# Two chunks of the up projection multiplied before the layer norm ahead of them, and corrected afterwards

## What is computed

```
x = layer_norm(x, ln_in_g, ln_in_b)
for l in range(2):
    ...                                           # four mixers side by side give ym
    x = layer_norm(ALPHA * x + (1 + g1) * (ym @ w_out[l]), ln1_g[l], ln1_b[l])
    h = x * (1 + sc2) + sh2
    a = depthwise_conv3(h @ w_up[l], conv_w[l]) + conv_b[l]     # w_up: 1024 x 5632
    val, gate = split(a)
    x = layer_norm(ALPHA * x + (1 + g2) * ((val * silu(gate)) @ w_down[l]), ln2_g[l], ln2_b[l])
```

## Time and profile before

| | |
|---|---|
| median of three runs | 1433.19 us |
| profiled execution | 1431.97 us |
| its span, first to last instruction | 1429.9 us |
| TensorE busy | 1358.1 us, 95% |
| VectorE, ScalarE, GpSimd busy | 772.3, 505.8, 537.4 us |
| mean granted TensorE clock | 0.965 |

### The profile page before, as it was taken

One profiled execution on the slowest core, in us unless ns is written; L12 is line 12 of the kernel. 1 busy time (PEld: TensorE's weight loads), 2 busy tenths in 40 slices (PEclk: granted clock), 3 DMA queues, 4 the chain that ended last, 5 costly groups with the idle time before them and its releaser, 6 DMA issues.

```text
span 1429.9 us, 17219 instructions
## 1 busy us (share of the span) xinstructions
PE 1358.1 (95%) x6876; PEld 1013.5 (71%) x6876; DVE 772.3 (54%) x1366; ACT 505.8 (35%) x762; POOL 537.4 (38%) x325
## 2 busy tenths in 40 slices
PE   6999999999999999899899999999999999989987
PEld 3445676787888888688665577677788888868865
DVE  5985778646676676432468655664533333321135
ACT  2523225335333333332242422343543333333222
POOL 0630100575444444344346110056544444434431
PEclk9998999999999999999999999999999999999998
DMA  9356732032565555454224441102133333222311
GB/s 382 148 118 163 174 124 90 16 103 90 181 200 190 186 184 179 160 182 156 106 64 118 85 81 30 45 16 88 59 89 103 89 92 100 89 73 90 102 59 59
DMA packets 64799, 166.78 MB, mean 117 GB/s; under 512 B 14288, under 2 KB 26960, under 8 KB 64208
## 3 DMA queue, kind: packets, MB, share of 16 engines
q1 hardware_dynamic: 64720, 165.68, 38.1%
HBM read 160.04 MB, written 5.62 MB: 116 GB/s over the span
## 4 chain that ended last, share of the span: by engine, by line
PE 79%; DVE 14%; issue 3%; DMA 2%; POOL 1%; ACT 1%; SPq 1%; ACTq 0%; POOLq 0%
PE bank L449 19%; PE bank L451 19%; PE bank L450 19%; PE bank L530 6%; PE bank L524 3%; PE bank L555 2%; PE bank L464 2%; PE bank L469 1%; DVE scr L1237 1%; DVE xa L1044 1%; PE bank L683 1%; DVE xa L1038 1%; DMA s_w<-scr 1%; PE bank L458 1%; PE bank L692 1%
## 5 line engine op out<-in xcount | busy, mean ns | idle before, releaser
L2083 POOL TENSOR_TENSOR ring_r<-ring,scr_r 128x1024 fp32r<-128x1024 f32 x148 | 360.2, 2435 | 442.0 <-ACT scr_r L1950 272.8
L449 PE MATMUL bank<-ym_r,scr_r 128*128 128x512 f32 x704 | 280.2, 398 | 5.1 <-DVE hm_r L1600 4.1
L451 PE MATMUL bank<-hm_r,scr_r 128*128 128x512 f32 x704 | 279.4, 397 | 0.0
L450 PE MATMUL bank<-ym_r,ring_r 128*128 128x512 f32 x704 | 276.7, 393 | 0.0
L449 PE MATMUL bank<-scr_r 128*128 128x512 f32 x480 | 197.2, 411 | 28.7 <-issue 14.2
L450 PE MATMUL bank<-scr_r,ring_r 128*128 128x512 f32 x480 | 191.3, 399 | 0.0
L1616 DVE SCALAR_TENSOR_TENSOR scr<-bank,pb,scr 128x511 f32<-128x511 f32 x88 | 66.0, 750 | 211.9 <-ACT scr L1943 211.8
L530 PE MATMUL bank<-hm,ring 128*128 128x512 f32 x352 | 171.7, 630 | 0.0
L1099 DVE SCALAR_TENSOR_TENSOR ada<-ada,silu_c 128x1024 f32<-128x1024 f32 x80 | 134.2, 1680 | 50.5 <-DMA ada<-in_w_ada 50.5
L449 PEld LDWEIGHTS bank<-ym_r,scr_r 128*128 128x128 f32 x704 | 132.3, 188 | 38.7 <-issue 5.7
L451 PEld LDWEIGHTS bank<-hm_r,scr_r 128*128 128x128 f32 x704 | 132.3, 188 | 33.0
(11 more groups left out here) (332 smaller groups left out, 1791.2 us busy)
## 6 DMA issues: line engine op xcount, KB each, us to landing
ring<-in_w_up SPq DMA_DIRECT2D x88, 512.0 KB, 3.7
ada<-in_w_ada SPq DMA_DIRECT2D x80, 512.0 KB, 3.7
ring<-in_w_down SPq DMA_DIRECT2D x44, 512.0 KB, 3.6
ring<-in_w_in SPq DMA_DIRECT2D x34, 512.0 KB, 4.5
scr<-in_w_ada SPq DMA_DIRECT2D x16, 512.0 KB, 14.5
ring<-in_w_out SPq DMA_DIRECT2D x16, 512.0 KB, 4.2
pa<-in_par_a SPq DMA_DIRECT2D x2, 2144.5 KB, 12.9
xa<-in_x SPq DMA_DIRECT2D x1, 2048.0 KB, 8.3
```

Source lines behind the costliest of these rows:

```text
L449: first = mm(dst, w_hi, x_hi, start=start, stop=False)
L450: mm(dst, w_lo, x_hi, start=False, stop=False)
L451: return first, mm(dst, w_hi, x_lo, start=False, stop=stop)
L2083: G.tensor_tensor(ring_r[:, at, :], ring[:, at, :], high[:, at, :].bitcast(F32), ALU.subtract)\
```

## The change

The product with w_up is linear in h, and h = (xa * rstd - mean * rstd) * g + b for each frame. So a chunk of it can be made from the stream as it is ahead of the norm, times g, and corrected later: multiplied by the spread row rstd, less the spread row mean * rstd times the column sums of g * w, plus the column sums of b * w.

- `zh` (ScalarE) and `z_low` (VectorE) split xa * g into its two halves, a slice at a time, right behind `residual`. The square of each slice comes behind `zh`, and `z_low` waits for that square.
- `weigh` (VectorE) multiplies up chunks 0 and 1 by g and by b, after slice 5; `collect` adds the eight slices of each: chunk 0 after slice 6, ahead of residual 7; chunk 1 ahead of `norm_apply`. GpSimd makes the low part of these two chunks, in place, only after `weigh` has read them.
- TensorE runs `norm_stats`, raw slices 0 and 1 of the pair, the spreads, raw slices 2 to 6, four one-column matmuls for the sums, raw slice 7. All `keep_awake` of this norm are gone. Then chunks 2 and 3 form the pair that goes slice by slice as h comes.
- ScalarE makes the high part of up chunk 3 ahead of the norm's square root, copies the raw results out of banks 2 and 3 between h's slices 2, 3 and 4, and makes those of chunks 4 and 5 among and behind h's slices.
- VectorE makes the low part of chunk 4 and the corrections behind `norm_apply`; ScalarE adds one bias instruction ahead of the first tap of each raw chunk.

```diff
+                def raw_slice(k):
+                    pe.wait_ge(S["raw_step"], l * NRAW + RAW[f"z{k}"])
+                    for r, (w_hi, w_lo) in enumerate(raw_pair):
+                        first, last = thrice(banks[2 + r][:, :], w_hi[:, k, :], w_lo[:, k, :], zh[:, k, :],
+                                             z_low_tile(k), k == 0, k == KD - 1)
+                        if k == 0 and r == 0:
+                            first.then_inc(S["chunk_used"], 1)
...
+                for k in range(KD):
+                    pe.wait_ge(S["h_lo_odd" if k % 2 else "h_lo"], l * (KD // 2) + k // 2 + 1)
+                    for r, (w_hi, w_lo) in enumerate(pair):
+                        first, last = thrice(banks[4 + r][:, :], w_hi[:, k, :], w_lo[:, k, :], ym_r[:, k, :],
+                                             hm_r[:, k, :], k == 0, k == KD - 1)
+                        if k == 0 and r == 0:
+                            first.then_inc(S["chunk_used"], 2)
...
+                def z_low(k):
+                    v.wait_ge(S["ln_sq"], (2 * l + 1) * KD + k + 1)
+                    V.scalar_tensor_tensor(z_low_tile(k), xa[:, k, :], gh[:, 1, 0, k:k + 1], zh[:, k, :].bitcast(F32),
+                                           ALU.mult, ALU.subtract).then_inc(S["raw_step"], 1)
+                def weigh(r):
...
+                    for x in range(2):
+                        ins = V.tensor_tensor(weighed[r][:, x, :, :], ring[:, slot(l, n), :].rearrange("p (k m) -> p k m", m=P),
+                                              gh[:, 1, x, :].rearrange("p (k o) -> p k o", o=1).to_broadcast([P, KD, P]), ALU.mult)
+                    ins.then_inc(S["raw_step"], 1)
+                def collect(r):
+                    a = weighed[r]
+                    ch.link(V.tensor_tensor(a[:, :, 0:4, :], a[:, :, 0:4, :], a[:, :, 4:8, :], ALU.add))
+                    ch.link(V.tensor_tensor(a[:, :, 0:2, :], a[:, :, 0:2, :], a[:, :, 2:4, :], ALU.add))
+                    V.tensor_tensor(columns[:, r, :, :], a[:, :, 0, :], a[:, :, 1, :], ALU.add).then_inc(S["raw_step"], 1)
...
                     norm_square((2 * l) * KD, m, m)
+                weights_high(l, KD + 3)
                 norm(2 * l + 2)
...
+                    if k in (2, 3):
+                        a.wait_ge(S["up_mm"], l * (2 * KF) + 2)
+                        A(up_raw[:, k - 2, :], banks[k][:, :], ACT.Identity)
+                    if k == 5:
+                        weights_high(l, KD + 4)
+                weights_high(l, KD + 5)
...
+                    if q in (KD, KD + 1):
+                        g.wait_ge(S["raw_step"], l * NRAW + RAW[f"weighed{q - KD}"])
```

More of the change, by code:

```diff
@@ L109 @@
 TAIL = 4
+RAW = {name: i + 1 for i, name in enumerate(
+    [f"z{k}" for k in range(6)] + ["weighed0", "weighed1", "z6", "sum0", "z7", "sum1", "low", "up0", "up1"])}
+NRAW = len(RAW)
 PA = [("gm_g", GW), ("gm_b", GW), ("gm_ws", HEADS * P), ("gm_bs", CT * P),
@@ L495, in norm_stats, with norm_pause @@
                     last.then_inc(S["ln_bcast"], 1)
+            def norm_pause(n, late=None):
+                norm_stats(n, late)
+                keep_awake(1)
+                norm_spread(n)
                 keep_awake(2)
@@ L508, in _ @@
             last.then_inc(S["ln_accq"], 1)
-            norm_stats(1)
+            norm_pause(1)
             for l in range(L):
@@ L959, in _ @@
                 pe.wait_ge(S["up_conv"], l * (2 * KF) + 2)
[L960 to L965, removed]
+                pe.wait_ge(S["resid"], (2 * l) * KD + 5)
+                raw_pair = [parts(l, FIRST_UP + r) for r in range(2)]
+                def raw_slice(k):
[3 more added lines that the diff above has]
+                                             z_low_tile(k), k == 0, k == KD - 1)
                         if k == 0 and r == 0:
@@ L1594, in _ @@
                     sum_x(2 * l, m, range(KD))
+                    z_low(m)
+                    if m == 5:
+                        weigh(0)
+                        weigh(1)
+                    if m == 6:
+                        collect(0)
                 V.memset(small[:, 90:91], 0.0).then_inc(S["mixers_done"], 1)
@@ L1601, in h_low @@
                         .then_inc(S["h_lo"], 1)
-                norm(2 * l + 2, h_low)
+                norm_var(2 * l + 2)
+                norm_rstd(2 * l + 2)
+                collect(1)
+                norm_apply(2 * l + 2, h_low)
+                at4 = slot(l, FIRST_UP + 4)
+                v.wait_ge(S["w_hi"], l * NSPLIT + KD + 5)
+                V.tensor_tensor(ring_r[:, at4, :], ring[:, at4, :], wh[:, at4, :].bitcast(F32), ALU.subtract)\
+                    .then_inc(S["raw_step"], 1)
+                v.wait_ge(S["up_mm"], l * (2 * KF) + 1)
+                ch.post(V.tensor_scalar(st[:, 20:22], banks[7][:, 72:74], -1.0, None, ALU.mult))
+                ch.post(V.tensor_scalar(st[:, 22:24], banks[7][:, 74:76], 1.0, None, ALU.mult))
+                v.wait_ge(S["h_hi"], l * KD + 5)
+                for r in range(2):
+                    ch.post(V.tensor_tensor(up_raw[:, r, :], up_raw[:, r, :], banks[0][:, :], ALU.mult))
+                ch.settle()
+                for r in range(2):
+                    V.scalar_tensor_tensor(up_raw[:, r, :], banks[1][:, :], st[:, 20 + r:21 + r], up_raw[:, r, :],
+                                           ALU.mult, ALU.add).then_inc(S["raw_step"], 1)
                 v.wait_ge(S["parb_in"], 16 * l + 16)
```

90 lines of the change are left out of this document (72 added, 18 removed).

## The result

Four runs took 1451.38 us in the median (1448.03 to 1455.52), against 1432.83 of the kernel before on the same chip: a ratio of 1.0148, 95% interval 1.0108 to 1.0189. The forecast was 1452 us. The profiled execution took 1455.52 us, the slowest of the four, with a span of 1453.7, 23.8 us more than before; between the two medians lie 18.6 us.

The account below looks back on a forecast made before the run. TensorE, busy 95% of the span, was taken as the bound. Two layers at +8.6 us plus 2.5 us behind the pair made 19.7 us on the profiled 1431.97 us: 1452 us, range 1434 to 1461.

Parts of the forecast that it names:

- Residual 7 late, TensorE standing still behind it: At the norm: VectorE's queue starts residual 7 near 331.8 instead of 320.51; sums end 11.5 us late, TensorE idle.
- the slip of slices 0 to 5: VectorE's queue before weighing starts late and stays about 2.5 us behind; slice 5's z_low ends near 314.9.
- The root behind a landing: ScalarE's square root waits for chunk 3's load, high part and table load; root and reciprocal done at 343.8.
- From the spreads to the pair's end: Spreads, raw slices, column sums, then chunks 2 and 3 without waiting: ends at 366.1 against 357.5, +8.6 us per layer.
- Behind it: First convolution chunks after the pair: waits for late low parts and a load behind a modulation load, +2.5 us over both layers.
- B: Rival: VectorE's instructions fall between GpSimd's, half the turns stay away, residual 7 about 5 us earlier; 1442 us, chance 0.14.
- C: Rival: no turns that matter, sums end at 325.9, root still waits for the landing; 1431 us, no change, chance 0.12.
- D: Rival: works as intended, VectorE keeps up and the root isn't held, -5.0 us in each layer; 1422 us, chance 0.05.
- E: Rival: waits pile up in the convolution's first chunks, or GpSimd's running sum comes last; 1465 us, chance 0.07.

Follow-up runs that it names:

- e2: The changed kernel without the weigh and collect work on VectorE (column sums set to zero, that correction left out): ratio 1.0042 to the kernel before.
- e9: The kernel before with only weigh and collect added on VectorE, GpSimd's low parts waiting for them, results unused: ratio 1.0094 to the kernel before.
- e6: The changed kernel with chunk 0 weighed behind slice 5, chunk 1 behind slice 6, chunk 0 collected behind residual 7: ratio 1.0121 to the kernel before.
- e1: The changed kernel with ScalarE's high part of up chunk 3 moved behind the norm's square root: ratio 1.0095 to the kernel before.
- e5: The changed kernel with every modulation load of layer 0 one place later in SyncE's queue: ratio 1.0321 to the kernel before.
- e12: The changed kernel with only modulation loads 2 to 7 of layer 0 one place later in SyncE's queue: ratio 1.0118 to the kernel before.
- e3: The changed kernel without weigh and collect, and with the root ahead of chunk 3's high part: ratio 0.9985 to the kernel before.
- e4: The changed kernel with weigh and collect replaced by VectorE instructions of about the same time, one operand in PSUM: ratio 1.0117 to the kernel before.
- e11: The changed kernel with column sums made on TensorE, the root first, and e12's later modulation loads: 1426.99 us, ratio 0.9976 to the kernel before.

## Why the prediction was right, step by step

*Residual 7 late, TensorE standing still behind it.* Right, and shown by e2 and e9. Residual 7 was forecast 11.5 us behind the mark and came at 10.3, the sums were forecast 11.5 us late and were 10.1 (10.5 in layer 1). The walk itself, from the first `weigh` to residual 7, was forecast at 16.9 us, 9.4 of it undisturbed instructions and 7.3 turns; it took 16.6, with 7.2 of turns, and each turn is where it was placed (in the second pair of `weigh`, in `z_low` 6, in `collect`). What was over by 1.1 us is the slip of slices 0 to 5: `weigh` began at 313.84, not 314.9. What the forecast left out is TensorE's wait for the low parts ahead of `norm_stats`, 4.28 us; it cost nothing only because residual 7 was later, and e6 shows it as the next limit.

*The root behind a landing.* Right in mechanism: 6.9 us from the sums to the root, forecast 6.9. What it costs was taken as what the raw slices don't cover, some 2 us; e1 shows 4, since the sum had the clock at full behind the wait.

*From the spreads to the pair's end.* From the reciprocal to the end of raw slice 7 the forecast had 11.2 us at full clock, measured were 12.8 from the start of the spreads, 3.4 of them at half clock. So this term was 1.6 us short in each layer, about as much as the sums were over: raw slice 7 was forecast to end at 355.0 and ended at 354.8. Chunk 4 was forecast to start at 366.1 and started at 366.2; TensorE's waits show none of 0.3 us or more in the pair. To here the change costs 8.8 and 9.0 us in the layers, forecast 8.6.

*Behind it.* The term that was mis-sized: +2.0 us in layer 0, measured 5.9 (5.8 of it in chunks 4 to 7: the wait of 3.62, half clock for some 3 us behind it, the rest small), and +0.5 in layer 1, measured nothing. A weight load behind a modulation load is in the rows, and the modulation row itself met GpSimd's turn, 3.04 us instead of 1.22. But e5 and e12 give back only 3 of the 5.8, so this mechanism is about half of the term; the cause of the rest stays open.

*The rivals.* B (fewer turns, 1442) lay outside the interval. C rested on no turns and falls with the 2.71 us of a 0.69 us sum. D, 1422, was said to need residual 7 in time and the root off the landing's path; e3 has both and comes to 0.9985 of before, not to 0.993, since layer 0's tail and the late sums (7.4 us behind the mark, not 4.6) remain. E didn't come: only chunk 7 waited long.

The errors went both ways, and that 1452 us met a median of 1451.38 is partly luck. Against the profiles the sum was 3.9 us short of 23.6: 1.4 and 1.0 too much for the sums in the two layers, 1.6 too little for the clock in each, 3.9 too little behind the pair in layer 0, 0.6 too much in layer 1. The median itself is of four runs that lie 7.5 us apart.

## What to carry to other kernels

Before filling TensorE's pause with early work, count what the preparation puts in front of the instruction that ends the pause, and on which engine: here 9.4 us of VectorE's instructions, undisturbed, ahead of one residual of 0.75 us that TensorE waited for. Read a queue not only for its busy share over the program, but in the stretch itself and together with the engine that it takes turns with: over the program before, VectorE was busy 54% and GpSimd 38%, but in the 16.6 us ahead of residual 7 in the changed kernel they were busy 16.1 and 13.1 us, turns included. And an instruction that waits for a landing doesn't belong ahead of one on the critical path, least of all where that load is released by work behind that same path.

## What the runs showed of the hardware that I had not expected

A second fall of the clock: back at full 5.0 us after the first raw slice had started at half, TensorE paused 2.05 us, the clock stayed at 1.00 during the pause, and fell to 0.50 during the spreads that followed it. The same fall followed each of the nine pauses of 1.93 to 2.67 us ahead of the spreads (both layers of the changed kernel, e4, e5 and e6, layer 1 of e12). It did not follow the pauses of 1.66 (e12, layer 0), 1.82 and 1.78 us (e2) at this place, nor before the pause of 2.15 us, which lies ahead of the pair's large matmuls. What decides is open.

VectorE and GpSimd alternate instruction by instruction even where VectorE's come back to back: a sum of 128x256 took 0.43 us in one kernel and 2.45 in another.

The part of the program ahead of the out projection, which none of these edits touches, varies between executions, and the mark with it: in layer 0 it came between 314.8 and 321.0 us (without the three kernels that have new matmuls ahead of it, the same range). A single profile of each kernel would have mistaken up to 6 us of that for an effect. The stretches between marks are better but not free of it: same code in layer 1 repeated within 0.2 us in three kernels and within 2.1 in three others, and in layer 0 of e12 and e11 a clock that didn't fall gave 1.7 and 3.1 us that the edit had not made.
